# Weighted rows written twice by ScalarE, lower parts taken by the pair, and a split in two halves

## What is computed

```python
def rms_norm(x, w):
    xf = x.astype(F32)
    y = xf * lax.rsqrt(jnp.mean(xf * xf, axis=-1, keepdims=True) + EPS)
    return (y * w.astype(F32)).astype(x.dtype)
...
    for layer in range(DEPTH):
        h = rms_norm(x, norm_w[layer, 0])
        ...
        x = x + rms_norm(m, norm_w[layer, 1])
        f, buf = conv_ffn(rms_norm(x, norm_w[layer, 2]), conv_states[layer], ...)
        x = x + rms_norm(f, norm_w[layer, 3])
```

## Time and profile before

| | |
|---|---|
| median of 3 runs | 2670.43 us (2670.35 to 2671.95) |
| the profiled execution, own time | 2670.63 us |
| its span in the trace | 2668.8 us |
| granted TensorE clock, mean over the span | 0.999 |
| TensorE busy | 2658.8 us of the span |
| VectorE busy | 1762.1 us |
| ScalarE busy | 1303.2 us |
| GpSimd busy | 403.8 us |

### The profile page before, as it was taken

How to read it: one execution, slowest core, us unless ns; L and a number is a source line. 1 busy time by engine, 2 the same in 40 slices (tenths; PEclk the granted TensorE clock), 3 DMA queues, 4 the chain that set the end, 5 groups by cost and what they waited for, 6 DMA issues and landing times.

```text
span 2668.8 us, 55312 instructions
## 1 busy us (share of the span) xinstructions
PE 2658.8 (100%) x19765; PEld 2638.9 (99%) x19765; DVE 1762.1 (66%) x2911; ACT 1303.2 (49%) x2181; POOL 403.8 (15%) x792
## 2 busy tenths in 40 slices
PE   9999999999999999999999999999999999999999
PEld 9999999999999999999999999999999999999998
DVE  7888888848776534666645855548766535767644
ACT  6565665545444333444444566545444334444443
POOL 2111111101322100222200000002323001222200
PEclk9999999999999999999999999999999999999999
DMA  6444444444545555454555422344544555444553
GB/s 237 146 140 136 143 135 139 132 167 146 176 160 166 162 166 167 161 167 160 162 168 175 151 89 85 119 160 146 177 163 165 161 167 168 159 167 163 161 166 120
DMA packets 123253, 413.66 MB, mean 155 GB/s; under 512 B 13920, under 2 KB 20480, under 8 KB 123168
## 3 DMA queue, kind: packets, MB, share of 16 engines
q1 hardware_dynamic: 115056, 406.37, 46.8%
q10 hardware_dynamic: 7056, 3.21, 0.4%
q0 software_dynamic: 1056, 2.92, 0.3%
HBM read 406.97 MB, written 5.48 MB: 155 GB/s over the span
## 4 chain that ended last, share of the span: by engine, by line
PE 97%; DVE 2%; ACT 0%; issue 0%; DMA 0%; DVEq 0%; SPq 0%; ACTq 0%
PE bank L278 30%; PE bank L280 30%; PE bank L279 30%; PE bank L1891 1%; PE bank L907 1%; PE bank L868 1%; PE bank L875 0%; PE bank L908 0%; PE bank L1896 0%; DVE w_lo L272 0%; PE bank L1251 0%; DVE cv L1451 0%; PE bank L910 0%; PE bank L362 0%; DVE cv L1449 0%
## 5 line engine op out<-in xcount | busy, mean ns | idle before, releaser
L272 DVE TENSOR_TENSOR w_lo<-raw,w_hi 128x1024 fp32r<-128x1024 f32 (+2 forms) x772 | 936.0, 1223 | 439.0 <-ACT w_hi L265 438.7
L278 PE MATMUL bank<-h_hi,w_hi 128*128 128x288 f32 (+1 forms) x4072 | 1220.3, 300 | 1.7 <-DVE h_lo L1231 1.1
L279 PE MATMUL bank<-h_lo,w_hi 128*128 128x288 f32 (+1 forms) x4072 | 1208.2, 297 | 0.0
L280 PE MATMUL bank<-h_hi,w_lo 128*128 128x288 f32 (+1 forms) x4072 | 1204.8, 296 | 0.0
L265 ACT ACTIVATE w_hi<-raw 128x1024 fp32r<-128x1024 f32 (+2 forms) x772 | 792.3, 1036 | 816.7 <-PE bank L280 812.8
L278 PEld LDWEIGHTS bank<-h_hi,w_hi 128*128 128x128 f32 x4072 | 763.1, 187 | 4.4 <-issue 2.8
L280 PEld LDWEIGHTS bank<-h_hi,w_lo 128*128 128x128 f32 x4072 | 766.7, 188 | 0.2
L279 PEld LDWEIGHTS bank<-h_lo,w_hi 128*128 128x128 f32 x4072 | 764.6, 188 | 0.7
L1503 POOL TENSOR_TENSOR ext<-yt,small 128x256 f32<-128x256 f32 x176 | 211.4, 1201 | 1489.9 <-ACT yt L1368 1024.1
L278 PE MATMUL bank<-g_hi,w_hi 128*128 128x288 f32 x1408 | 416.8, 296 | 0.0
L279 PE MATMUL bank<-g_lo,w_hi 128*128 128x288 f32 x1408 | 415.4, 295 | 0.0
(11 more groups left out here) (301 smaller groups left out, 2321.3 us busy)
## 6 DMA issues: line engine op xcount, KB each, us to landing
raw<-in_w_fi SPq DMA_DIRECT2D x352, 512.0 KB, 4.1
raw<-in_w_hi_in SPq DMA_DIRECT2D x128, 512.0 KB, 4.0
raw<-in_w_fo SPq DMA_DIRECT2D x128, 512.0 KB, 3.5
raw<-in_w_fo SPq DMA_DIRECT2D x64, 384.0 KB, 3.5
raw<-in_w_ho SPq DMA_DIRECT2D x32, 512.0 KB, 4.0
raw<-in_w_mo SPq DMA_DIRECT2D x32, 512.0 KB, 3.9
raw<-in_w_down SPq DMA_DIRECT2D x18, 512.0 KB, 4.5
raw<-in_w_ukv SPq DMA_DIRECT2D x16, 512.0 KB, 3.7
```

The lines of the kernel that those rows point to most:

```text
L272: dve.tensor_tensor(lo, raw[:, ch.slot, 0:ch.units * P], hi.bitcast(F32), ALU.subtract).then_inc(lo_done, 1)
L278: pe.matmul(out, top[:, w], rhs_hi, start=start, stop=False)
L279: pe.matmul(out, top[:, w], rhs_lo, start=False, stop=False)
L280: return pe.matmul(out, rest[:, w], rhs_hi, start=False, stop=stop)
```

## The change

ScalarE writes each weighted row of the seven pairs a second time, in plain fp32, into Y (new semaphore `n_full`). VectorE then takes the lower parts of both rows of a pair in one subtraction, Y minus H_HI (`lower_pair`), after the add of the next group. Since Y now holds the weighted rows, the squares can only be written when the lower parts are taken (they wait on `h_ready`), and ScalarE's loop makes them six groups later: the groups 0, 1 and 2 within its last three steps, the groups 3 to 8 behind the loop. The lower part of the fifth chunk is taken in two halves, one where it was, one behind `add(2)`. TensorE executes 12 fillers instead of 13.

```diff
+        def split_lo_part(dve, phase, k, part):
+
+            ch = Chunk(phase, 0, k)
+            half = slice(part * UNITS // 2 * P, (part + 1) * UNITS // 2 * P)
+            hi, lo = split_weights(ch)
+            if part == 0:
+                dve.wait_ge(hi_done, ch.number + 1)
+            op = dve.tensor_tensor(lo[:, half], raw[:, ch.slot, half], hi[:, half].bitcast(F32), ALU.subtract)
+            if part == 1:
+                op.then_inc(lo_done, 1)
...
-            split_next(eng, split, phase, (4,) if more else (3,))
+            if more and split is split_lo:
+                split_lo_part(eng, NEXT[phase], 4, 0)
+            else:
+                split_next(eng, split, phase, (4,) if more else (3,))
...
-                for k0, n in row_groups(s):
+                groups = row_groups(s)
+
+                def squares(k0, n):
+                    act.wait_ge(h_ready, KT * s + k0 + n)
+                    act.activation(Y[:, k0:k0 + n, :], X[:, k0:k0 + n, :], ACT.Square).then_inc(x_squared, n)
+
+                for g, (k0, n) in enumerate(groups):
                     rows = range(k0, k0 + n)
                     for k in rows:
                         act.wait_ge(x_ready, KT * (s - 1) + k + 1)
                         act.activation(H_HI[:, k, :], X[:, k, :], ACT.Copy, scale=norm_w[:, lb_, wb, k:k + 1]).then_inc(n_hi, 1)
-                    act.activation(Y[:, k0:k0 + n, :], X[:, k0:k0 + n, :], ACT.Square).then_inc(x_squared, n)
+                    if n == 2:
+                        for k in rows:
+                            act.activation(Y[:, k, :], X[:, k, :], ACT.Copy, scale=norm_w[:, lb_, wb, k:k + 1]).then_inc(n_full, 1)
                     for k in rows:
                         if k in EARLY[s]:
                             split_hi(act, NORM_OF[s], 0, EARLY[s][k])
+                    if g >= 6:
+                        squares(*groups[g - 6])
+                for g in range(len(groups) - 6, len(groups)):
+                    squares(*groups[g])
...
-                keep_busy(pe, 13)
+                keep_busy(pe, 12)
...
+            def lower_pair(k0):
+                rows = slice(k0, k0 + 2)
+                dve.wait_ge(n_hi, KT * s + k0 + 2)
+                dve.wait_ge(n_full, (KT - 2) * (s - 1) + k0)
+                dve.tensor_tensor(H_LO[:, rows, :], Y[:, rows, :], H_HI[:, rows, :].bitcast(F32), ALU.subtract)\
+                    .then_inc(h_ready, 2)
+                if k0 + 1 in EARLY[s]:
+                    split_lo(dve, NORM_OF[s], 0, EARLY[s][k0 + 1])
...
             lower(0)
-            for g in range(2, len(groups)):
-                k0, n = groups[g - 1]
+            scale(2)
+            lower(1)
+            add(2)
+            split_lo_part(dve, NORM_OF[s], 4, 1)
+            for g in range(3, len(groups)):
                 scale(g)
-                lower(k0)
                 add(g)
-                for c in range(k0 + 1, k0 + n):
-                    lower(c)
-            for c in range(groups[-1][0], KT):
-                lower(c)
+                lower_pair(groups[g - 1][0])
+            lower_pair(groups[-1][0])
```

More of the change, by code:

```diff
@@ L218, in trunk_program @@
         x_squared, x_summed = sem("x_squared"), sem("x_summed")
-        n_hi, h_ready = sem("n_hi"), sem("h_ready")
+        n_hi, n_full, h_ready = sem("n_hi"), sem("n_full"), sem("h_ready")
         STAT = 5
```

## The result

| | before | changed |
|---|---|---|
| median (lowest to highest) | 2670.39 us (2670.11 to 2671.95, 4 runs) | 2686.93 us (2686.26 to 2687.82, 4 runs) |
| profiled execution, own time | 2670.63 us | 2686.26 us |
| its span | 2668.8 us | 2684.4 us |
| granted clock, mean | 0.999 | 0.998 |

The changed kernel is slower: ratio 1.0062, 95% interval 1.0049 to 1.0074, that is 16.5 us. The forecast was 2682.5 in a range of 2680 to 2690.

The account below looks back on a forecast made before the run. TensorE was taken as the bound, busy throughout. The sum's release, 4.0 us later per norm with gains and row stalls contained in it, gave 12.0 over three norms: 2670.63 to 2682.6, about 2682.5 as median; range 2680 to 2690.

Parts of the forecast that it names:

- TensorE is the bound, and a wait is added one for one: Whole run: TensorE is busy throughout, 97% of the last chain, so any wait it gets adds fully to the end.
- The start: Each norm's first row: half a split and one filler fewer let it start 0.27 us earlier, 0.8 in all.
- The supply of rows: VectorE's lower parts in each norm's rows: pairs replace singles, subtraction 0.75 us; stalls make a norm 0.9 longer.
- The wait at row 2: Each norm's row 2: TensorE waits 0.8 us for its lower part, since the pair's subtraction needs four ScalarE copies.
- TensorE's own path to chunk 8: Through each norm's rows up to the sum: TensorE arrives 0.9 us later than before by its own path.
- the wait at the sum: TensorE's sum of the rows, ahead of chunk 9: a wait of 3.1 us per norm for VectorE's sum of squares.
- The sum of VectorE's queue: VectorE's steps in a norm's rows, added up: the last pair of X is ready 0.3 us earlier.
- ScalarE's queue: Behind each norm's last rows: two copies and late pairs of squares put the next split, then the sum, 4.0 us later.
- the main case: The forecast as worked out, for the whole run: 2680 to 2686 us, likeliest 2682.5, chance 0.75.
- The one of the clock: Rival: the clock falls in TensorE's new wait at each norm's sum; +7 us, 2689.7, chance 0.18.
- The rival that ended at no change: Rival: squares are done when TensorE asks for their sum; only start and rows count, 2669.7 to 2673.2, chance 0.07.
- a sign of the wrong mechanism: In the profile after: the prediction is wrong if ScalarE is seen to square while it used to idle.

Follow-up runs that it names:

- e5: The changed kernel with 12 fillers on TensorE ahead of its wait for the sum in each norm; 2684.01 us, ratio 1.0051.
- e1: The kernel before with only the fifth chunk's lower part in two halves and 12 fillers for 13; 2671.10 us, ratio 1.0003.
- e2: The kernel before with only ScalarE's squares made six groups later, no copies or pairs of lower rows; 2681.89 us, ratio 1.0046.
- e3: The changed kernel with the squares two groups late in place of six; 2677.47 us, ratio 1.0026.
- e6: The changed kernel with the squares four groups late in place of six; 2681.65 us, ratio 1.0041.
- e4: The changed kernel with TensorE's sum of the rows behind chunk 9 in place of chunk 8; 2681.42 us, ratio 1.0042.
- e9: e3 with VectorE's sum of squares moved between its two next splits; 2675.41 us, ratio 1.0020.
- e8: e3 with rows 2 and 3 not copied in fp32 and their lower parts taken singly; 2677.71 us, ratio 1.0028.

## Why the prediction was right, point by point

*TensorE is the bound, and a wait is added one for one.* Right. The offset between the two traces grows at the three norms and stays between them, but for 0.5 us twice: the kernel before waits 0.44 at a split some 23 us behind the first sum, and the same behind the third. e5, as late at the sums but with no fall of the clock, has this wait too; the changed kernel, which the fall has made later still, does not. That takes back part of each fall: some 1.5 us lost (14 matmuls at 0.24 in place of 0.13), 1.0 kept.

*The start.* Right, slightly oversized: the first row came 0.21, 0.26 and 0.20 us earlier, for 0.27 each. The first scaling began 0.09 behind the root. What was wrong is how much it is worth: e1 shows that the half put off costs more in the rows than this gain. I had costed the second half as part of VectorE's queue, and did not ask what it does to TensorE in rows 4 to 10.

*The supply of rows.* The pair's subtraction took 0.75, as I chose, and the copy 0.52. The wait at row 2 was 0.79, for 0.8. TensorE's own path to chunk 8 was undersized: it came 1.5, 1.8 and 1.5 us later than before, where I had 0.9, since row 2, counted from start to start, costs 1.05, since rows 8 and 10 together cost 0.3 where I had under 0.1 each, and since in the second norm chunk 8 waited 0.3 for its own lower part. As the working said, this is contained in the wait at the sum, which was 2.9 in place of 3.1. The sum of VectorE's queue was mis-sized: I had the last pair of X 0.3 us earlier, and it came at 637.26, 23.20 behind the norm's start, where it was 23.03: 0.17 later. The term is the add right behind its scale. I gave 0.03 for the semaphore (the line in the earlier trace rows gives 0.04); here the add starts at 622.03, 0.10 behind the scale's end (621.18 + 0.75), so a pair's scale holds the engine for 0.85 and not 0.78. Six times 0.07 is 0.4 of the 0.5 missing; the start is the rest.

*ScalarE's queue.* From the last pair's arrival to the split I had 0.87 + 0.86 + 4.0 = 5.73; it is 643.03 - 637.29 = 5.74. The term that it rests on is the copy, for which I had 0.52, holding the engine for 0.43 when another follows; two of them took 0.95 together, which is 0.43 + 0.52.

*The time.* The measured 2686.9 lies above the 2680 to 2686 of the main case: it is in the range only because the range was stretched to 2690 for the clock. The chain from the squares to the sum is as forecast, and the runs show it; that two short terms, the norms by 1.6 and the clock, left out of the likeliest case, by 2.9, did not carry the time past the range is in part luck. Without the falls of the clock (e5) it is 2684.0, inside the main case. For the norms I had 4.0 each, 12.0 in all, against 4.46, 4.79, 4.38 and 13.6. The missing 0.5 of a norm is the dependent adds. In the second norm one more add, that of the last pair, began 0.47 after VectorE had fallen idle, where it is about 0.1 in the others; why, no run tells.

*The rivals.* The one of the clock came true beside the main case, not in place of it. I gave it 0.18; what spoke for it was only the end of the run, where the granted clock is 0.51. No run shows the term behind its 2689.7, 2.4 for each norm. That was my estimate from one opening: the sixteen fillers there took 6.49 us, 2.4 over the 4.1 that they would take at 0.26 each, and I put that down to the clock. But the granted clock of the first 9 us is 1.00 in every trace here, and the same sixteen fillers took 5.52 us in the changed kernel, and from 5.34 to 6.58 over all traces. What the runs showed in its place is 1.0 net for each fall, in two norms of the profiled execution, and probably in all three of two others. The clock was 0.51 and 0.52 behind the first and the third of its waits of 2.8 us, and 1.00 behind the second: so short a wait was enough twice, and once it was not. With the falls at their measured price the forecast would have been about 2685. The rival that ended at no change is refuted: the sum did not keep up, because ScalarE's order is the program's (e2, e3, e6). I gave as a sign of the wrong mechanism that ScalarE squares while it used to idle; in e3, where it does, the time is indeed 9.5 us less.

*What I had not seen.* That moving TensorE's sum out of the way would not help in the ConvFFN (e4). The prediction spoke of a release that sets the time "whatever comes before"; it should have said that all engines start the next stage from this sum's root.

## What to carry to other kernels

When work is put off on an engine that has idle time, look where the idle time lies: here it was all in front of the point to which the squares were moved, and each of them came out on the critical path at its full price, 0.57 us for a pair of rows. Before moving a wait on the bound engine out of the way, ask what else starts from the same event; if it is the next stage's feeder, making the event earlier helps (e9, 2.0 us less than e3, each against its own kernel before) and waiting for it later does not (e4, 4.9 us of waits for a lower part where the changed kernel has 0.3). And an engine that is busy throughout a stretch has no place for half a split, even if the whole one seemed to be in the way (e1: 0.25 us gained at the start, 0.5 lost in the rows).

## What the hardware showed that I had not expected

The clock fell, to 0.50, also behind a wait well under those of the changed kernel. In e6 TensorE waited 2.0 us at the third sum (1846.55), and then (same columns as above):

```profile
1848.00:1851.40 3.40, 3.40 (x16) 3.40 (x15) 1.45 (x2) 2.66 (x3) 2.85 (x8) 0.50 0.68 202
```

It did not fall (1.00) behind that kernel's waits of 2.0 and 2.3 in the first two norms, nor in the changed kernel behind the second norm's 2.9, nor in e2 behind the second and third of its three waits of 2.9. In e8's opening it fell behind a wait of 1.79 us:

```profile
9.01 0.38 PE L289 MATMUL bank<-h_hi,w_hi 128*128 128x288 f32 x1 [1.79 <-DVE h_lo L1257]
```

```profile
9.25:12.50 3.25, 3.25 (x15) 3.25 (x15) 2.92 (x7) 3.25 (x7) 1.90 (x4) 0.50 1.03 422
```

The granted clock is 1.00 up to 9.25 and again from 12.75, while the changed kernel's own opening, with 2.57, has no fall. So waits of 2.0 and of 2.9 us had both outcomes, and executions of one kernel differ by 1 us or more for it. In each of the five falls TensorE was already at work again, for 0.2 to 1.5 us, when the clock went down (0.2 in e8, 1.5 in e6). Still, where fillers stand in these waits, in e5, it is 1.00 behind all three sums, and the mean is 1.0 in all four runs.

And a VectorE instruction that needs the result of the one right before it started behind its end, in the two kinds seen here, where the next independent one started 0.08 to 0.09 before it (in the changed kernel the pair's subtraction at 622.71, the add before it ending at 622.79). For the add behind a pair's scale (576 elements) the distance is 0.10 us; for the last step of the sum of squares, also behind 576 elements, it is 0.04. So the width alone does not set it, and no run here says what does.
